# Second cross attention: keys and values made in the third layer's sparse pairs; memory loaded first; feature chunks by one-column products

## The reference

```python
for layer in range(2):                                    # first block
    mod = silu(c) @ ada_w[layer] + ada_b[layer]           # 6 x 1024: shift, scale, gate, twice
    sh1, sc1, g1, sh2, sc2, g2 = split(mod, 6)
    h = rms_norm(x, norm1_g[layer]) * (1 + sc1) + sh1
    x = x + g1 * (even_mixer(h) if layer == 0 else odd_mixer(h))
    h = rms_norm(x, norm2_g[layer]) * (1 + sc2) + sh2
    x = x + g2 * grouped_moe(h)
for layer in range(2):                                    # second block
    y = even_mixer_2(h) if layer == 0 else diff_mixer(h)  # forget + sparse heads, or differences
    x = x + rms_norm(y, g[1])
    mem_n = rms_norm(mem, mem_norm_g[layer])
    k, v = mem_n @ ca_wk[layer], mem_n @ ca_wv[layer]     # 1024 x 256 each
    x = x + rms_norm(cross_attention(rms_norm(x, g[2]), k, v) , g[3])
    x = x + rms_norm(swiglu(rms_norm(x, g[4])), g[5])
```

## Time and profile before

| | before |
|---|---|
| median of three runs | 1932.01 us |
| lowest, highest | 1924.81, 1933.83 us |
| the profiled execution | 1938.03 us |
| its span | 1936.2 us |
| PE busy | 1807.3 us (93%) |
| DVE busy | 1264.0 us (65%) |
| ACT busy | 1072.8 us (55%) |
| mean granted clock of PE | 0.962 of 2.4 GHz |
| transfers | 413.09 MB, 213 GB/s |

### The profile page before, as it was taken

How to read it: one execution, slowest core, us unless ns; L and a number is a source line. 1 busy time by engine, 2 the same in 40 slices (tenths; PEclk the granted TensorE clock), 3 DMA queues, 4 the chain that set the end, 5 groups by cost and what they waited for, 6 DMA issues and landing times.

```text
span 1936.2 us, 27184 instructions
## 1 busy us (share of the span) xinstructions
PE 1807.3 (93%) x9604; PEld 1494.8 (77%) x9604; DVE 1264.0 (65%) x2000; ACT 1072.8 (55%) x1649; POOL 13.8 (1%) x29
## 2 busy tenths in 40 slices
PE   5998899999999999999999999988999998889998
PEld 4785478888886866888888678676999876669997
DVE  5686658889885766589889652755544565555454
ACT  2443247878873364578878552555444454554443
POOL 1000000000000000000000000000000000000000
PEclk9998889999999999899999998889999999989999
DMA  9866638899993845399899653122656561215652
GB/s 351 298 237 228 202 125 314 323 356 357 322 352 135 314 131 174 120 352 356 324 355 355 224 158 118 44 88 66 186 184 195 166 207 54 88 44 175 194 177 85
DMA packets 217285, 413.09 MB, mean 213 GB/s; under 512 B 13120, under 2 KB 69488, under 8 KB 216800
## 3 DMA queue, kind: packets, MB, share of 16 engines
q1 hardware_dynamic: 214176, 400.74, 60.2%
q0 software_dynamic: 1904, 8.26, 1.3%
q10 hardware_dynamic: 1120, 2.97, 0.4%
HBM read 410.87 MB, written 1.05 MB: 213 GB/s over the span
## 4 chain that ended last, share of the span: by engine, by line
PE 80%; DVE 10%; ACT 5%; issue 2%; DMA 2%; DVEq 0%; ACTq 0%; SPq 0%
PE banks L722 21%; PE banks L724 20%; PE banks L723 20%; PE banks L739 2%; DVE weights_low L2071 2%; PE banks L984 2%; PE banks L1126 2%; DMA weight_ring<-in_ada_w 2%; PE banks L1069 1%; DVE row_gains L2342 1%; PE banks L752 1%; ACT scratch L1671 1%; PE banks L923 1%; PE banks L779 1%; PE banks L875 1%
## 5 line engine op out<-in xcount | busy, mean ns | idle before, releaser
L2071 DVE TENSOR_TENSOR weights_low<-weight_ring,weights_high 128x1024 fp32r<-128x1024 f32 (+1 forms) x656 | 771.8, 1218 | 186.7 <-ACT weights_high L1520 106.5
L722 PE MATMUL banks<-weights_high,features_parts 128*128 128x512 f32 (+1 forms) x1488 | 590.8, 397 | 19.4 <-DVE features_parts L2504 8.2
L724 PE MATMUL banks<-weights_high,features_parts 128*128 128x512 f32 (+1 forms) x1488 | 581.1, 391 | 0.0
L723 PE MATMUL banks<-weights_low,features_parts 128*128 128x512 f32 (+1 forms) x1488 | 581.0, 390 | 0.0
L1800 ACT ACTIVATE weights_high<-weight_ring 128x1024 fp32r<-128x1024 f32 x384 | 391.1, 1055 | 102.4 <-PE banks L724 72.7
L722 PEld LDWEIGHTS banks<-weights_high,features_parts 128*128 128x128 f32 x1488 | 281.3, 189 | 84.4 <-DVE weights_low L2071 16.3
L724 PEld LDWEIGHTS banks<-weights_high,features_parts 128*128 128x128 f32 x1488 | 280.9, 189 | 59.4
L723 PEld LDWEIGHTS banks<-weights_low,features_parts 128*128 128x128 f32 x1488 | 281.2, 189 | 55.4 <-issue 1.0
L1520 ACT ACTIVATE weights_high<-weight_ring 128x1024 fp32r<-128x1024 f32 (+1 forms) x176 | 176.0, 1043 | 139.3 <-PE banks L724 85.5
L722 PE MATMUL banks<-features_parts,weights_high 128*128 128x256 f32 x736 | 210.5, 286 | 1.1 <-DVE features_parts L2166 1.0
L723 PE MATMUL banks<-features_parts,weights_high 128*128 128x256 f32 x736 | 208.4, 283 | 0.0
(11 more groups left out here) (371 smaller groups left out, 1620.2 us busy)
## 6 DMA issues: line engine op xcount, KB each, us to landing
weight_ring<-in_exp_w_gate SPq DMA_DIRECT2D x128, 512.0 KB, 5.0
weight_ring<-in_exp_w_up SPq DMA_DIRECT2D x128, 512.0 KB, 5.0
weight_ring<-in_exp_w_down SPq DMA_DIRECT2D x128, 512.0 KB, 5.1
weight_ring<-in_ada_w SPq DMA_DIRECT2D x96, 512.0 KB, 5.6
weight_ring<-in_ffn_wg SPq DMA_DIRECT2D x44, 512.0 KB, 4.1
weight_ring<-in_ffn_wu SPq DMA_DIRECT2D x44, 512.0 KB, 4.7
weight_ring<-in_ffn_wd SPq DMA_DIRECT2D x44, 512.0 KB, 4.2
weight_ring<-in_even_w_in SPq DMA_DIRECT2D x28, 512.0 KB, 5.7
```

What stands on the lines that cost most here:

```text
L722: eng.matmul(dst, lh, rh, start=first, stop=False, **kw)
L723: eng.matmul(dst, lh, rl, start=False, stop=False, **kw)
L724: mm = eng.matmul(dst, ll, rh, start=False, stop=last, **kw)
L2071: V(half_of(low(s), i, size), half_of(slot(n), i, size), half_of(high(s), i, size).bitcast(F32), ALU.subtract)\
```

## The change

- **Memory first.** SyncE loads half of chunk 0 and waits for the memory before it goes on; GpSimd's small loads wait for it too. VectorE sums half of chunk 0, normalises the memory, and then sums the other half.
- **Second cross attention.** Its keys and values leave the start. The memory is loaded again while layer 1's experts begin, squared and scaled on ScalarE there, turned by TensorE behind the experts' loop in place of eight fillers, and copied with the gain into two thirds of `row_gains`. Its two weight matrices go through the ring between the third layer's input and output projections. In each opening sparse item of the third layer, eight fp32 products (`mem_second`) go in front of the item's own; ScalarE copies the result when the item closes. The gains for that layer are loaded only after the last of them.
- **Splits.** `AHEAD` for `b0` becomes 0, 10 and 12. The first projection's second tile is split halfway through the turn (`midway`), not before it.
- **Feature chunks.** 1, 3, 9, 12, 13, 14 and 15 are made on TensorE by 32 one-column products each (weights stationary, `c` moving); 10 goes to VectorE's sums. The multiply and reduce become one addition. Chunk 12 is loaded ahead of 11.
- **Late loads.** The gate bias joins the relative bias, cos/sin and decay, and all of them wait for the first group of the first projection.

```diff
-ADA_ON_PE = (10, 12, 14)
+ADA_ON_PE = (1, 3, 9, 12, 13, 14, 15)
+ADA_LOADS = [*range(11), 12, 11, *range(13, 24)]
+A0_CHUNKS = [7, 8, *ADA_LOADS[9:16]]
...
-        AHEAD = {"b0": (0, 1, 12), "b1": (0, 1, 8)}
+        AHEAD = {"b0": (0, 10, 12), "b1": (0, 1, 8)}
...
+            first = st["ada"][0]
+            load(first[0], cols(a["ada_w"][0], 0, 512, 0, 4), 4)
+            eng.wait_ge(mem_loaded, 16)
+            eng.dma_start(MEM_WEIGHTS[0], cols(a["ca_wk_2"][0], 0, 256)).then_inc(kv_loaded[0], 16)
+            load(first[1], cols(a["ada_w"][0], 0, 512, 4, 4), 4)
+            loaded_chunks[0] += 1
+            ada()
+            eng.dma_start(MEM_WEIGHTS[1], cols(a["ca_wv_2"][0], 0, 256)).then_inc(kv_loaded[1], 16)
+            ada(2)
...
+            for i, w in enumerate(("ca_wk_2", "ca_wv_2")):
+                load(st["mem1"][i], cols(a[w][1], 0, 256), KD)
             stream("ev_out", a["ev_w_out_2"][0], D)
...
-                    for k in range(4):
-                        at = 4 * i + k
-                        mm = eng.matmul(B[bank][:, :], CF[:, at:at + 1].to_broadcast([128, 128]), w[:, k, :],
-                                        start=at == 0, stop=at == KD - 1)
+                    for i in range(4):
+                        for k in range(4):
+                            mm = eng.matmul(bank[:, 4 * x + i:4 * x + i + 1], w[:, k, i * 128:(i + 1) * 128],
+                                            CF[:, 4 * x + k:4 * x + k + 1], start=k == 0, stop=k == 3)
...
                         joins = d["kind"] == "nsa"
+                        if joins and d["opens"]:
+                            mem_second(d["p"], o)
...
+            def mem_second(p, bank):
+
+                values, i = divmod(p, 2)
+                t = st["mem1"][values]
+                loaded(t)
+                steps = mem_steps(1, slot(t).rearrange("p (k n) -> p k n", k=KD), i, values)
+                for k, (left, right) in enumerate(steps):
+                    mm = eng.matmul(bank[:, 256:512], left, right, start=k == 0, stop=k == KD - 1)
+                if i:
+                    mm.then_inc(*used.up())
...
+                if l == 1:
+                    eng.wait_ge(mem_normed, 1)
+                    eng.wait_ge(backs_copied, 5 * l + 5)
+                    for k in range(KD):
+                        for tb in range(TB):
+                            at = (k % 2) * S + tb * 128
+                            mm = eng.transpose(B[(2, 3, 6, 7)[k // 2]][:, at:at + 128],
+                                               MEM_ROWS[tb][:, k * 128:(k + 1) * 128], ident)
+                    mm.then_inc(mem_turned, 1)
+                stay_busy(2, 0 if l else 8)
...
-            def take_turned(name, dst, affine=None, split=False):
+            def take_turned(name, dst, affine=None, split=False, midway=None):
...
+                    if midway is not None and i == 3:
+                        midway()
...
+                    eng.wait_ge(mem_again, 16 * TB)
+                    for tb in range(TB):
+                        square(PR[:, 2048 + D * tb:2048 + D * (tb + 1)], MEM_ROWS[tb], 4 + tb)
+                    eng.wait_ge(squares, sq[0])
+                    eng.activation(ROOT[:, 4:6], SS[:, 4:6], ACT.Sqrt, scale=1.0 / D, bias=EPS_[:, :]).then_inc(root_ready, 1)
...
-            splits(tiles[st["even_in"][0][0][0]]["split"] + 2)
+            s0 = tiles[st["even_in"][0][0][0]]["split"]
+            splits(s0 + 1)
             eng.wait_ge(scales_ready, 1)
...
-                        rows = lambda ap: ap.rearrange("p (i f) -> p i f", i=4)
-                        V(rows(room), rows(bank), wide(ident.unsqueeze(1), 128, 4, 128), ALU.mult).then_inc(*vec.up())
-                        settle()
-                        eng.tensor_reduce(to, rows(room), AX.X, ALU.add).then_inc(*vec.up())
+                        V(to, bank[:, 4:8], new, ALU.add).then_inc(*vec.up())
...
-            eng.wait_ge(copied["act"], chunks[st["kv1"][1][-1]]["done"])
+            eng.wait_ge(copied["act"], chunks[st["even_in"][0][1][1]]["done"])
+            eng.dma_start(GB[:, 0:2, :], a["gate_bias"][0:2].partition_broadcast(128)).then_inc(gates_loaded, 16)
...
+                if l == 0:
+                    eng.wait_ge(weights_used, tiles[st["mem1"][1]]["order"] + 1)
                 for i in range(3):
                     eng.dma_start(GB[:, i, :], a["sandwich_g_2"][l, 2 * i + 1, :].partition_broadcast(128))\
```

More of the change, by code:

```diff
@@ L136, in cross @@
         st[f"cao{l}"] = (t, [p.chunk(t, i == 3, "dve") for i in range(4)])
-    for l in range(2):
-        p.turn(f"mem{l}", KD)
-        st[f"kv{l}"] = []
-        for _ in range(2):
-            ada(1)
-            st[f"kv{l}"].append([p.chunk(None, False, "act") for i in range(2)])
+    p.turn("mem0", KD)
+    ada(4)
+    st["kv0"] = [[p.chunk(None, False, "act") for i in range(2)] for _ in range(2)]
     p.turn("a0h1", KD)
@@ L165, in make_plan @@
         group("ev_in", "act", min(512, EV_IN - 512 * j))
+    st["mem1"] = p.tiles_of(2, split=False)
     p.turn("b0sparse", 8)
@@ L272, in build @@
         B = [PS[:, i, :] for i in range(8)]
-        ADA_ON_DVE = [j for j in range(24) if j not in ADA_ON_PE]
+        ADA_ON_DVE = [j for j in ADA_LOADS if j not in ADA_ON_PE]
         def ada_sum(j):
@@ L1145, in _ @@
             turns_taken("mem0")
-            mem_keys(0)
-            turn("mem1", lambda i, tb: NB[:, tb, i * 128:(i + 1) * 128])
-            turns_taken("mem1")
-            modulation((2, 3))
-            mem_values(0)
-            modulation((2, 3))
-            mem_keys(1)
-            modulation((2, 3))
-            mem_values(1)
-            modulation((2, 3))
+            mem_first(0)
+            for _ in range(2):
+                modulation((2, 3))
+            mem_first(1)
+            for _ in range(2):
+                modulation((2, 3))
             eng.wait_ge(mod_taken, 4)
-            eng.wait_ge(copied["act"], chunks[4]["done"])
+            eng.wait_ge(copied["act"], chunks[0]["done"])
             eng.wait_ge(fill_ready, 1)
@@ L1792, in experts @@
                 high_gathered(5 * l)
+                if l == 1:
+                    eng.wait_ge(mem_rooted, 1)
+                    for tb in range(TB):
+                        ins = eng.activation(MEM_ROWS[tb], MEM_ROWS[tb], ACT.Copy, scale=RSD[:, 4 + tb:5 + tb])
+                    ins.then_inc(mem_normed, 1)
                 with eng.Fori(0, PASSES) as p:
@@ L2597, in _ @@
                 ada_take(j, (2, 3))
-            splits(tiles[st["even_in"][0][0][0]]["split"] + 2)
+            s0 = tiles[st["even_in"][0][0][0]]["split"]
+            splits(s0 + 1)
             eng.wait_ge(scales_ready, 1)
-            take_turned("a0h1", feature, lambda i: (SCL[:, 0, i:i + 1], MOD[:, 0, i:i + 1]), True)
+            take_turned("a0h1", feature, lambda i: (SCL[:, 0, i:i + 1], MOD[:, 0, i:i + 1]), True, lambda: splits(s0 + 2))
             eng.wait_ge(more_loaded, MORE)
```

136 lines of the change are left out of this document (72 added, 64 removed).

## The result

| | before | after |
|---|---|---|
| median | 1930.05 us (4 runs) | 1980.91 us (4 runs) |
| lowest to highest | 1924.81 to 1933.83 | 1978.17 to 1984.73 |
| ratio of the two | | 1.026 (95% interval 1.0231 to 1.0288) |
| profiled execution | 1938.03 us | 1984.73 us |
| PE busy | 1807.3 us | 1859.2 us |

The medians are 50.9 us apart, the two profiled executions 46.7. The profiled execution of the kernel before was a long one of its kind, and one stage shows it: from the output projection of layer 0 to the first expert product of layer 1 it took 565.1 us, and 561.2 in the changed kernel. The change touches nothing there, and two later kernels that are equal to the one before in that stage took 560.9 and 562.1.

A forecast was written before the change was run, and what follows sets the result against it. The prediction took TensorE, 80% of the chain that ended last, as the bound. Its terms 6 + 1 + 21 + 18 made +46 us: 1984 profiled, 1978 against the median, range 1942 to 1994.

The forecast's parts named there:

- Start: Kernel's start: memory lands near 10, turns begin near 14, the layer's feature turn begins at 61.8 us instead of 62.10.
- the choice on which most of the sum hung: One-column products: 2.5 us at the high clock, the rest at the low one, 11.7 us a chunk.
- The sign that the prediction named: In the start, the 64 records of chunk 1's products would take over 11 us, not 7.5.
- Tile 9 and the projection: First projection: TensorE waits 6.5 us for the second tile's low part, second group near 89.5; +6 us.
- the 1 us for the late loads: First projection: gate bias, relative bias, decay and cos/sin moved behind the first group cost +1 us, bounds 0 and 4.
- Attention: Layer 0's chunk attention: 29 us more TensorE work, less 8 us of its waits on VectorE; +21 us.
- Pairs: Third layer's sparse pairs: memory products exposed, 14.3 us, split at step 10 +3, split at step 12 +1; +18 us.
- Covered: Layer 1's experts: the added squares, root, turns and copies fit into idle time; uncovered, 5 us in all.
- B: One-column products in start and attention: the clock holds through busy narrow stretches; +11 us, 1943 us; chance 0.17.
- D: Attention and pairs: TensorE takes all added products in its idle time at full clock; -3 us, 1922 to 1929; chance 0.08.
- C: Third layer's pairs absorb the memory products, +4 instead of +18, the rest as forecast; +32 us, 1964 us; chance 0.12.
- E: Whole kernel: low clock all through, with late loads and tile 12 colliding; +65 us, 1997 us; chance 0.05.

The follow-up runs named there:

- the run of form against form: Changed kernel, its seven feature chunks made by eight 512-column products each instead of 32 one-column ones; 2035.53 us, ratio 1.0564, a whole time the study calls unusable.
- the run of all edits: Changed kernel: chunks 1 and 3 on VectorE, five by 512-column products, second tile's low part earlier, memory products before the wait, relative bias later; 1931.75 us.
- the run with one product of eight: Changed kernel with seven of the eight memory products left out of each opening sparse item of the third layer; 1966.42 us, ratio 1.0202.
- the run of three edits: Changed kernel: chunks 1 and 3 on VectorE, second tile's low part before chunk 4's sums, memory products before the wait for copies; 1957.42 us, ratio 1.0132.

## Why the forecast held

The forecast of +46 for the profiled execution met +46.7, and that closeness is partly luck. By stage it told +7 up to the attention, +21 in it and +18 in the pairs; measured were +8.7, +18.5 and +23.2. Those make 50.4, near the 50.9 of the medians, and the stage in which the kernel before was 3.9 us long for no cause of the change brings them down. The mechanisms are the ones that it named; the sizes are gone through here.

**Start.** The memory landed at 8.7 and the turns began at 13.0 (forecast near 10 and 14). The narrow chunks fell from the high level to the low one in the middle of a busy stretch, which was the choice on which most of the sum hung. In the changed kernel TensorE has no pause in either of these windows (as the earlier trace rows):

```profile
29.00:31.00 2.00, 2.00 (x20) 2.00 (x20) 0.14 (x1) 0.00 (x0) 0.00 (x0) 1.00 1.03 374
33.00:37.00 4.00, 4.00 (x20) 4.00 (x20) 2.24 (x3) 0.00 (x0) 0.00 (x0) 0.50 0.69 253
```

A chunk took 9.6 and 12.2 us there, and 52.9 / 5 = 10.6 in the attention, where 11.7 was taken: the step was right and its size off by a tenth. At the two rates the 9.62 us are 42 records at 0.117 and 22 at 0.213, not 21 and 43, so the clock stayed up for some 5 us in chunk 1; in chunk 3 it was under 2 us, some 15 records. The sign that the prediction named, over 11 us for chunk 1, did not come, and that for the attention's clock did (0.62). The turn began at 60.4 (forecast 61.8) and the first product at 67.6 (near 70). From the turn to the first product it is 7.2 us instead of 7.8: TensorE's waits of 0.51 and 0.69 us between the turns are gone, which the forecast had not counted. I take the cause to be the second tile's splits, which no longer stand ahead of the turn's copies. (The prediction's sum for an attention all at the low clock gives 71.3 and not 71.8, which changes no figure behind it.)

The Trainium skill (TensorE: Matmul & The Clock Gate, Part 1) has the clock fall with idleness and released by sustained busyness. The trace does not agree: the second window is as gapless as the first and runs at half the rate, and with 512-column products in the same place TensorE's clock stayed at 1.00.

**Tile 9 and the projection.** Forecast: a wait of 6.5 us and the second group at 89.5, so +6, with +1 for the late loads. Measured: a wait of 6.75, the second group at 87.35 (+4.1), and then a wait of 4.23 before the third group that was not foreseen; +8.7 at the projection's end. The term that is too small is the 1 us for the late loads: behind the second group another 4.6 us were lost. One link of it the traces show, the transfers in the first group (the last two columns; the kernel before, then the changed one):

```profile
70.00:80.00 10.00, 10.00 (x47) 8.27 (x46) 7.85 (x13) 4.82 (x8) 0.98 (x2) 1.00 0.80 269
```

```profile
70.00:80.00 10.00, 3.31 (x15) 2.42 (x13) 8.79 (x13) 0.63 (x1) 0.00 (x0) 0.84 0.01 2
```

While the low part of the second tile is late, its ring slot is taken, SyncE waits for it for up to 15.7 us, and the transfers stand at 0.01 where they were at 0.80. Then the loads that were missed and the 3.4 MB of late loads come together, and the transfers are full from 80 on. With the low part first the same 10 us are at 0.58, and the third group is still only 0.95 us earlier, so this gap is not all of it. How much the late loads take is not shown; in the kernel before, moving 1.5 MB of them away changed nothing.

**Attention.** +21 forecast, +18.5 measured: TensorE 80.2 us busy (81.8), idle 8.5 (9.3), of which one wait is nearly all:

```profile
L893 PE MATMUL banks<-c_features,weight_ring 128*128 128x1 f32 x320 | 52.9, 302 | 0.1
L957 PE MATMUL banks<-constants,scratch 128*128 128x128 f32 x24 | 5.2, 377 | 8.2 <-DVE scratch L2309 8.2
```

That is chunk 10's sum ahead of the first pair's scaling, as the forecast had it. The reason given for the 29 us of added work, the loss of the high clock, is confirmed by the run of form against form and by the run of all edits. That the size came so near is in part luck, since this stage took 85.5 to 97.3 us in seven profiles.

**Pairs.** +18 forecast, +23.2 measured. TensorE, and VectorE's split, from the second opening item on:

```profile
1279.58 3.72 PE L1180 MATMUL banks<-row_gains,weight_ring 128*128 128x256 f32 x16 [1.07 <-ACT scratch L1716]
1290.13 3.72 PE L1180 MATMUL banks<-weight_ring,row_gains 128*128 128x256 f32 x16 [1.07 <-ACT scratch L1716]
1297.06 2.36 DVE L2126 TENSOR_TENSOR weights_low<-weight_ring,weights_high 128x1024 fp32r<-128x1024 f32 x2 [0.25 <-ACT weights_high L1556]
1300.35 1.01 PE L957 MATMUL banks<-constants,scratch 128*128 128x128 f32 x6 [2.81 <-DVE scratch L2309]
1303.28 6.54 PE L1180 MATMUL banks<-weight_ring,row_gains 128*128 128x256 f32 x16 [1.93 <-ACT scratch L1716]
...
1318.01 0.50 PE L736 MATMUL banks<-weights_high,features_parts 128*128 128x512 f32 x1 [3.17 <-DVE features_parts L2330]
```

The products cost 3.3 to 3.7 us per opening item at the high clock (forecast 3.6), and the last copy and split 0.5 (1). The third spacing grew by 8.86: 3.43 of products, 2.8 of low clock, and so 2.6 for the split at step 10 (3). Mis-sized is the fourth item: behind the waits of 2.81 and 1.93 us, the first of which the split makes, its 16 records ran at 1.2 GHz and took 6.54, 2.8 more. With that the sparse items sum to 19.8. The other 3.4 us lie ahead of the first opening item, where no instruction is new. TensorE is idle for 0.8 us there before and 0.9 in the changed kernel, and its clock is 0.80 and 0.75: this, too, is low clock, and the spread told of below.

**Covered.** The squares, root, turns and copies in layer 1's experts cost nothing: it takes 386.8 us from the experts' first product to the one behind the compression, and 387.4 before.

**Rivals.** B (the clock holds) and D (all is absorbed) are out by the windows above, and C (the pairs absorb the products) by the run with one product of eight. E (low clock all through) is out by the first of the two windows, at 1.00.

## What to carry to other kernels

Before you trade few wide products for many narrow ones, look in the trace for a long narrow stretch and its granted clock. The two forms cost nearly the same at 2.4 GHz here, by an estimate of 7.5 us a chunk and by 7.1 measured, and the difference was the clock, on the narrow products and on what stood behind them. Ask of a freed wait what lands next: where the transfers were over 0.85 busy, both memory first and the earlier split alone gave back half or more; only once the start was shorter did the same split gain 5.4 us (86.04 against 91.47 at the third group). Work moved from a full stage to one with idle time was hidden here only where it stood ahead of the wait, and at an even clock that hid the wait's length and no more (1.14 us for a wait of 1.07).

## What the hardware showed that was not expected

- The same narrow instructions fell to the low clock at another point in each profile. Layer 0's attention with its five narrow chunks took 85.5, 88.7, 88.9, 92.5, 92.6, 96.0 and 97.3 us in the profiles of seven kernels that are equal in this stage but reach it at other times, single chunks 8.7 to 13.7. With wide chunks (three of them, or five) it took 66.9 to 70.2 in five profiles. So a gain of 14.8 us ahead of it could end as 2.8.
- The clock differs in the same way ahead of the third layer's pairs, where there are narrow products of another kind. The same 29 records, in the run of three edits and in that of all, and the whole stretch from the product behind the compression to the first opening product, in the same order:

```profile
1212.53 3.62 PE L1413 MATMUL banks<-projected,qk_features 64*128 64x15 f32 x29
```

```profile
1190.41 5.54 PE L1413 MATMUL banks<-projected,qk_features 64*128 64x15 f32 x29
```

```profile
1196.09:1248.14 52.05, 51.26 (x327) 39.10 (x327) 31.66 (x132) 24.43 (x80) 0.00 (x0) 0.90 0.19 62
```

```profile
1171.54:1232.18 60.64, 59.85 (x325) 45.37 (x326) 29.43 (x130) 21.86 (x77) 0.00 (x0) 0.76 0.16 53
```

TensorE is idle for 0.8 us in both; the 8.6 us between them are its granted clock, 0.90 against 0.76, and the narrow records are 1.9 of them. From the product behind the compression to the first opening product it is 51.3 to 53.6 us in four profiles of kernels whose pairs are as before, and 52.1 to 60.7, with 3.5 of new products in it, in the eight that have the memory products there. What decides the clock from one execution to the next stays open.

- Some wide work among narrow products did not hold the clock: 14 products of 384 columns a chunk were pure cost, 29 us in all. How much would hold it was not tried.
